# Normed inputs of every stage: two tiles to an instruction on VectorE, scale and shift on ScalarE

## The reference

```python
def rms_norm(x, g):
    xf = x.astype(jnp.float32)
    y = xf * lax.rsqrt(jnp.mean(xf * xf, axis=-1, keepdims=True) + RMS_EPS)
    return (y * g.astype(jnp.float32)).astype(x.dtype)

def modulate(h, shift, scale):
    return h * (1 + scale[:, None, :]) + shift[:, None, :]
...
        h = modulate(rms_norm(x, norm_ffn1[l]), sh1, sc1)
        x = x + 0.5 * g1[:, None, :] * swiglu(h, ffn1_w_in[l], ffn1_w_out[l])
        h = modulate(rms_norm(x, norm_mix[l]), sh2, sc2)
        x = x + g2[:, None, :] * token_mix(h, cos, sin, mix_w_in[l], sgu_w[l], sgu_b[l], mix_w_out[l])
        h = modulate(rms_norm(x, norm_ffn2[l]), sh3, sc3)
        x = x + 0.5 * g3[:, None, :] * swiglu(h, ffn2_w_in[l], ffn2_w_out[l])
```

## Time and profile before

| | us |
|---|---|
| median of 3 runs | 2261.4 (2260.69 to 2261.54) |
| the profiled execution | 2257.29 |
| its span, first to last instruction | 2255.2 |
| TensorE busy | 2108.4 (93%) |
| VectorE busy | 1689.1 (75%) |
| ScalarE busy | 988.7 (44%) |

### The profile page before, as it was taken

How to read it: one execution, slowest core, us unless ns; L and a number is a source line. 1 busy time by engine, 2 the same in 40 slices (tenths; PEclk the granted TensorE clock), 3 DMA queues, 4 the chain that set the end, 5 groups by cost and what they waited for, 6 DMA issues and landing times.

```text
span 2255.2 us, 35615 instructions
## 1 busy us (share of the span) xinstructions
PE 2108.4 (93%) x15149; PEld 1947.6 (86%) x15149; DVE 1689.1 (75%) x2346; ACT 988.7 (44%) x1325; POOL 28.2 (1%) x33
## 2 busy tenths in 40 slices
PE   5999898999999999999999899999999998678998
PEld 4999887999999998799998678888888886568998
DVE  7899877788788876778776774777776667966664
ACT  3434444433343444453345664422222358754442
POOL 0000000000000000000000000000000001110000
PEclk7999998999999999999999999999999999888998
DMA  9899743698879965357774001255565141133662
GB/s 320 286 326 307 245 150 112 221 309 301 290 259 304 312 200 168 131 185 249 240 227 153 28 20 57 94 168 168 168 212 178 60 130 61 36 110 127 215 201 75
DMA packets 338629, 417.43 MB, mean 185 GB/s; under 512 B 9274, under 2 KB 263208, under 8 KB 338472
## 3 DMA queue, kind: packets, MB, share of 16 engines
q1 hardware_dynamic: 335072, 410.79, 55.2%
q10 hardware_dynamic: 3400, 4.38, 0.6%
HBM read 414.09 MB, written 1.05 MB: 184 GB/s over the span
## 4 chain that ended last, share of the span: by engine, by line
PE 45%; DVE 7%; ACT 3%; issue 2%; POOL 0%; DVEq 0%; ACTq 0%
PE pb L600 44%; ACT wh L1323 1%; DVE wl L1926 1%; DVE RS L2013 1%; PE pb L1168 1%; DVE ACC L1934 1%; DVE SM L2510 1%; DVE T L1934 1%; DVE L_y L1934 0%; DVE Hl L1934 0%; ACT A_P L1780 0%; DVE L_u L1934 0%; DVE Y L1934 0%; DVE T L1926 0%; DVE L_y L1926 0%
## 5 line engine op out<-in xcount | busy, mean ns | idle before, releaser
L600 PE MATMUL pb<-Hh,wh 128*128 128x256 f32 (+1 forms) x2624 | 797.3, 304 | 32.1 <-DVE Hl L1934 20.0
L600 PE MATMUL pb<-Hl,wh 128*128 128x256 f32 (+1 forms) x2624 | 782.1, 298 | 0.0
L600 PE MATMUL pb<-Hh,wl 128*128 128x256 f32 (+1 forms) x2624 | 781.8, 298 | 0.0
L1926 DVE TENSOR_TENSOR wl<-raw,wh 128x2048 fp32r<-128x2048 f32 (+3 forms) x271 | 601.3, 2222 | 198.0 <-ACT wh L1323 197.3
L1323 ACT ACTIVATE wh<-raw 128x2048 fp32r<-128x2048 f32 (+3 forms) x271 | 502.5, 1855 | 358.2 <-PE pb L600 285.9
L600 PEld LDWEIGHTS pb<-Hh,wh 128*128 128x128 f32 x2624 | 506.7, 193 | 52.4 <-issue 28.5
L600 PEld LDWEIGHTS pb<-Hl,wh 128*128 128x128 f32 x2624 | 506.6, 193 | 15.0 <-issue 2.2
L600 PEld LDWEIGHTS pb<-Hh,wl 128*128 128x128 f32 x2624 | 506.5, 193 | 12.8
L600 PE MATMUL pb<-Bh,wh 128*128 128x256 f32 (+1 forms) x1376 | 419.8, 305 | 7.5 <-DVE Y L1926 2.5
L600 PE MATMUL pb<-Bh,wl 128*128 128x256 f32 (+1 forms) x1376 | 413.1, 300 | 0.0
L600 PE MATMUL pb<-Bl,wh 128*128 128x256 f32 (+1 forms) x1376 | 413.1, 300 | 0.0
(11 more groups left out here) (245 smaller groups left out, 2003.3 us busy)
## 6 DMA issues: line engine op xcount, KB each, us to landing
raw<-in_ada_w_dram SPq DMA_DIRECT2D x128, 1024.0 KB, 5.6
raw<-in_ffn_w_in_dram SPq DMA_DIRECT2D x88, 1024.0 KB, 6.1
raw<-in_mlp_w_dram SPq DMA_DIRECT2D x64, 1024.0 KB, 5.3
raw<-in_ffn_w_out_dram SPq DMA_DIRECT2D x32, 1024.0 KB, 6.9
raw<-in_mix_w_in_dram SPq DMA_DIRECT2D x22, 1024.0 KB, 5.9
raw<-in_ffn_w_out_dram SPq DMA_DIRECT2D x16, 768.0 KB, 5.4
raw<-in_attn_w_qkv_dram SPq DMA_DIRECT2D x12, 1024.0 KB, 6.3
raw<-in_lru_w_in_dram SPq DMA_DIRECT2D x10, 1024.0 KB, 5.1
```

Source lines behind the costliest of these rows:

```text
L600: return e.matmul(o, l, r, start=st, stop=sp, skip_group_check=True)
L1926: return e.tensor_tensor(o, a, b, f)
```

## The change

`modulated` now works on pairs of tiles. VectorE multiplies two tiles of XC by RS in one instruction (RS is broadcast over the two). ScalarE then applies scale (the gain) and shift to each tile of T in place, one instruction each with two per-partition operands, and makes one high-half copy for both. VectorE subtracts that from T, one instruction for both, and raises h by 2. ScalarE's copy waits for ScalarE's own second instruction of the pair (act.step). Where no other work stands beside the tiles, the copy for tiles 2 and 3 is put off until tiles 4 and 5 are scaled, and the next one likewise. The callers now hand the gain to ScalarE's side. The form with two segments in one call, which had no caller left, is dropped. The eight context tiles of the first feed-forward stage (`c_high`, `c_low`) are as before.

```diff
-            def modulated(segs, apart=False, beside={}):
...
-                    E.wait_ge("h.t", E.up("h.t"))
-                    act(Hh[:, kt, c], T[:, kt, c], ACT.Identity, bias=b[:, kt:kt + 1]).then_inc(sems["h.hi"], 1)
-                E.up("h", len(order))
+            def modulated(c0, a, b, beside={}):
+                c, done = slice(c0, c0 + 256), []
+
+                def high():
+                    kt, v = done.pop(0)
+                    E.wait_ge("act.step", v)
+                    act(Hh[:, kt:kt + 2, c], T[:, kt:kt + 2, c], ACT.Copy).then_inc(sems["h.hi"], 1)
+
+                for kt in range(0, 8, 2):
+                    for k in (kt, kt + 1):
+                        for f in beside.get(k, ()):
+                            f()
                     E.wait_ge("h.t", E.up("h.t"))
+                    for k in (kt, kt + 1):
+                        v = E.step(act(T[:, k, c], T[:, k, c], ACT.Identity, bias=b[:, k:k + 1], scale=a[:, k:k + 1]))
+                    done.append((kt, v))
+                    if kt != 2 or beside:
+                        high()
+                while done:
+                    high()
+                E.up("h", 8)
...
-            def modulated(segs, apart=False):
...
-                    stt(Hl[:, kt, c], T[:, kt, c], b[:, kt:kt + 1], f32(Hh[:, kt, c]), ALU.add, ALU.subtract).then_inc(sems["h"], 1)
+            def modulated(c0):
+
+                c, waiting = slice(c0, c0 + 256), []
+                r = RS[:, c].unsqueeze(1).to_broadcast([128, 2, 256])
 
                 def low():
-                    kt, c, b, k = waiting.pop(0)
+                    kt, k = waiting.pop(0)
                     E.wait_ge("h.hi", k)
+                    tt(Hl[:, kt:kt + 2, c], T[:, kt:kt + 2, c], f32(Hh[:, kt:kt + 2, c]), ALU.subtract).then_inc(sems["h"], 2)
 
                 own()
...
-                    stt(T[:, kt, c], XC[:, kt, c], a[:, kt:kt + 1], RS[:, c], ALU.mult, ALU.mult).then_inc(sems["h.t"], 1)
-                    waiting.append((kt, c, b, E.up("h.hi")))
-                    if len(waiting) > 2:
+                for kt in range(0, 8, 2):
+                    tt(T[:, kt:kt + 2, c], XC[:, kt:kt + 2, c], r, ALU.mult).then_inc(sems["h.t"], 1)
+                    waiting.append((kt, E.up("h.hi")))
+                    if kt > 2:
                         low()
```

More of the change, by code:

```diff
@@ L1373, in root_mean @@
                     act(RS[:, c0:c0 + 256], p[:, c0:c0 + 256], ACT.Sqrt, bias=EPSC, scale=1.0 / D).then_inc(sems["rs.sqrt"], 1)
-            def modulated(segs, apart=False, beside={}):
-                order = [(kt, s) for kt in range(8) for s in segs] if not apart else [(kt, s) for s in segs for kt in range(8)]
-                for kt, (c0, b) in order:
-                    for f in beside.get(kt, ()):
-                        f()
-                    c = slice(c0, c0 + 256)
-                    E.wait_ge("h.t", E.up("h.t"))
-                    act(Hh[:, kt, c], T[:, kt, c], ACT.Identity, bias=b[:, kt:kt + 1]).then_inc(sems["h.hi"], 1)
-                E.up("h", len(order))
+            def modulated(c0, a, b, beside={}):
[8 more added lines that the diff above has]
+                            f()
+                    E.wait_ge("h.t", E.up("h.t"))
+                    for k in (kt, kt + 1):
[6 more added lines that the diff above has]
+                E.up("h", 8)
             def shift(b, v, l, s):
@@ L1425, in ffn @@
                     cx_ahead()
-                modulated([(0, shift(0, 0, l, seg))])
+                modulated(0, S_GAIN, shift(0, 0, l, seg))
                 if first:
@@ L1472, in mix @@
                     cx_ahead()
-                modulated([(0, shift(0, 0, l, 3))])
+                modulated(0, S_GAIN, shift(0, 0, l, 3))
                 if l:
@@ L1619, in root, with seam @@
                 act(RS[:, SEG[seg]], PB[bank][:, SEG[seg]], ACT.Sqrt, bias=EPSC, scale=1.0 / D).then_inc(sems["rs.sqrt"], 1)
-            def seam(second, b_x, b_c, squared, beside, between, behind=()):
+            def seam(second, x, c, squared, beside, between, behind=()):
                 root(SUMS_BANK, 0)
@@ L1718, in _ @@
             cx_ahead()
-            modulated([(0, shift(1, 1, 0, 0))])
+            modulated(0, S_GX, shift(1, 1, 0, 0))
             cx_ahead()
@@ L1822, in _ @@
             E.wait_ge("xn", 8)
-            seam(SUMS2[0], shift(1, 1, 0, 3), shift(1, 2, 0, 3), {3: (o2_out(4, 1),), 6: (lambda: ahead("o2"),)},
+            seam(SUMS2[0], (S_MX, shift(1, 1, 0, 3)), (S_MC, shift(1, 2, 0, 3)), {3: (o2_out(4, 1),), 6: (lambda: ahead("o2"),)},
                  {2: (lambda: ahead("m1"),), 4: (o2_out(6, 1),), 5: (o2_squares(1, 4, 5),), 6: (o2_squares(1, 6, 7),)},
@@ L1826, in _ @@
             mlp(512, [2] * 8, halves=True)
-            seam(SUMS2[1], shift(1, 1, 1, 0), shift(1, 2, 1, 0), {5: (lambda: ahead("m2"),)},
+            seam(SUMS2[1], (S_LX, shift(1, 1, 1, 0)), (S_LC, shift(1, 2, 1, 0)), {5: (lambda: ahead("m2"),)},
                  {2: (lambda: ahead("lg"),), 4: (y_squares(1, 0, 1),), 5: (y_squares(1, 2, 3),)},
@@ L1910, in _ @@
             root_mean(256)
-            modulated([(0, shift(1, 1, 1, 3))])
+            modulated(0, S_GC, shift(1, 1, 1, 3))
             mlp(256, [4] * 4)
@@ L2069, in ffn @@
                     mean_root(256)
-                modulated([(0, S_GAIN, shift(0, 0, l, seg))])
+                modulated(0)
                 if seg or l:
@@ L2130, in mix @@
                 mean_root(256)
-                modulated([(0, S_GAIN, shift(0, 0, l, 3))])
+                modulated(0)
                 if l:
@@ L2341, in y_half, with seam @@
                     E.mark(tt(y, y, p[:, :].rearrange("p (m n) -> p m n", m=2), ALU.add), "y")
-            def seam(gates, x, c, added, between, behind=()):
+            def seam(gates, added, between, behind=()):
                 add_normed(256, [(0, gates[0])])
@@ L2446, in _ @@
             mean_root(256)
-            modulated([(0, S_GX, shift(1, 1, 0, 0))])
+            modulated(0)
             cx()
@@ L2566, in _ @@
             gain(S_MC, 1, 2, 0, 3, ng(0, 2))
-            seam((S_OX, S_OC), (S_MX, shift(1, 1, 0, 3)), (S_MC, shift(1, 2, 0, 3)), (lambda: ahead("o2"),), (lambda: ahead("m1"),))
+            seam((S_OX, S_OC), (lambda: ahead("o2"),), (lambda: ahead("m1"),))
             mlp(512, [2] * 8, halves=True)
@@ L2572, in _ @@
             gain(S_LC, 1, 2, 1, 0, ng(1, 0))
-            seam((S_GX, S_GC), (S_LX, shift(1, 1, 1, 0)), (S_LC, shift(1, 2, 1, 0)), (lambda: ahead("m2"), lambda: y_half(0, 1)),
+            seam((S_GX, S_GC), (lambda: ahead("m2"), lambda: y_half(0, 1)),
                  (lambda: y_half(4, 1), lambda: ahead("lg"), lambda: ahead("lg")), (lambda: ahead("lg"), lambda: ahead("lg")))
@@ L2674, in _ @@
             mean_root(256)
-            modulated([(0, S_GC, shift(1, 1, 1, 3))])
+            modulated(0)
             mlp(256, [4] * 4)
```

15 lines of the change are left out of this document (4 added, 11 removed).

## The result

The changed kernel takes 2286.36 us (median of 4 runs, 2282.09 to 2290.98) against 2261.05 for the kernel before (4 runs, 2260.45 to 2261.54): a ratio of 1.0116, 95% interval 1.0104 to 1.0128. That is 25.3 us slower; 2286.7 had been predicted. The profiled execution is the slowest of the four: 2290.98, span 2288.9, so the trace shows 33.7 us more than the trace of before and not 25.3. The other three spans are 2280.0, 2280.4 and 2288.1.

A forecast was written before the change was run, and what follows sets the result against it. TensorE, busy 93%, was taken as the bound: only its waits and slowdowns count. Call terms 4.3 + 6.2 + 5.5 + 9.3 = 25.3 us, added to the median 2261.4, gave 2286.7; range 2273 to 2297.

The forecast's parts named there:

- What bounds the kernel: Whole kernel: TensorE is busy 93% of the span, so a microsecond counts only where it stands still or slows.
- The new rhythm: Each call: ScalarE sets the pace, holding 6.1 us; at 626 first tile 1.54 later, unit's end 2.3 later.
- low bound: All twelve calls with the scale operand free and no clock loss: together 17.4 us, 2279.
- TensorE's gap before the third tile: Call at 626: TensorE through two tiles at 4.80, then idle 1.06 until 5.86 after the first T.
- 418, 626, 977: Calls with TensorE at full clock, where the unit's end counts: 1.6, 2.3 and 2.3 us, sum 6.2.
- 39, 270, 2048: Calls with TensorE at half clock: start counts at the last two, ScalarE's queue at 39; 1.3, 1.5, 1.5, sum 4.3.
- 836, 1192, 1426, 1826: Calls where a later wait swallows TensorE's delay and its releaser sits behind VectorE or ScalarE: 1.4, 1.4, 1.4, 1.3, sum 5.5.
- 1401 and 1792: First halves of the seams: ScalarE's other work joins the chain; 4.5 and 4.8 us including half the clock loss, sum 9.3.
- Rival 3: Clock falls at 418, 626, 836, 977, 1192 and 1426, each with a 1.2 GHz spell: 2300, +39; chance 0.05.
- Busy times: Profile after: ScalarE's busy time rises by about 39 us, VectorE's falls by 26 us.
- The weighed page: Skill page on ScalarE: about 93 ns per per-partition operand, spacing 0.51 instead of 0.49, some 0.15 us more a call.
- Rival 2: All 12 calls: VectorE's time is what counts, 1.4 us less work each, so faster, 2244; chance 0.04.

The follow-up runs named there:

- the execution shown first: First profiled execution of the changed kernel, no further edit, set beside a second profiled execution of the same kernel: 2290.98 us, span 2288.9.
- the tile-by-tile kernel: Changed kernel with ScalarE's two passes kept, but each tile of 256 columns handled singly without waiting for a partner: 2281.86 us, ratio 1.0088.

## Why the prediction was right, and where it was not

- **What bounds the kernel: right.** VectorE's lighter load moved nothing; every delay is a wait for a tile or for what is queued behind it.
- **The new rhythm: right, to 0.06 us in all five times of the call at 626.** ScalarE holds some 6.1 us a call. The second operand measures 0.092 (588 to 496) against 0.09. The spacing of 0.49 that came from it was the term on which most hung, and the kernel without scale moved the total to +17.6 where the low bound had 17.4. Call by call it bears the terms out at 418, 626, 977 and 1401 (0.9, 1.7, 1.7, 3.2 against 1.0, 1.7, 1.7, 3.3), while 836 was 3.3 over its term and 270 2.2 under: the closeness of the total is partly luck.
- **TensorE's gap before the third tile: 0.74, not 1.06.** I had it through two tiles 1.44 after the start. By its rows it is through at 639.06 - 0.74 - 636.66 = 1.66, since the last matmul ends later than its successor could begin. No effect on the unit's end, 10.30.
- **418, 626, 977 (1.6, 2.3, 2.3): right**, 1.51, 2.34, 2.35, and 2.34 each where they stood alone.
- **39, 270, 2048 (1.3, 1.5, 1.5): the mechanism is half of it.** The first tile is 1.6 later, but the price is not. Clock at 2048, in the kernel before and in the changed one, from TensorE's first tile on:

```profile
2050.00:2053.00 3.00, 2.71 (x13) 2.75 (x14) 3.00 (x9) 1.87 (x5) 0.00 (x0) 0.50 0.00 0
2053.00:2055.00 2.00, 2.00 (x11) 2.00 (x11) 1.89 (x5) 1.72 (x3) 0.00 (x0) 0.50 0.00 0
2055.00:2057.00 2.00, 2.00 (x16) 2.00 (x16) 0.92 (x1) 1.05 (x1) 0.00 (x0) 0.83 0.00 0
```

```profile
2083.00:2086.00 3.00, 1.32 (x6) 1.36 (x7) 1.44 (x3) 2.97 (x7) 0.00 (x0) 0.50 0.00 0
2086.00:2088.00 2.00, 2.00 (x11) 2.00 (x11) 0.86 (x2) 2.00 (x5) 0.00 (x0) 0.50 0.00 0
2088.00:2090.00 2.00, 2.00 (x17) 2.00 (x16) 1.12 (x2) 2.00 (x2) 0.00 (x0) 0.88 0.00 0
```

  Full clock comes back 7.2 us after the first T in both (at about 2055.7 and 2088.5), whether TensorE began 1.8 or 3.4 after it. Who begins 1.6 later works 1.6 less at half clock and gets 0.7 back: 0.91, not 1.5. At 270 a refund of 0.4 is in the rows (from the first tile to the next wait 20.7 before, 20.3 now), and then two spells, from about 296 and from about 306, take some 2.9 (4.06 less the 1.2 by which that wait comes later): I had no term for them. At 39 the measured values, 1.4, 0.1 and 3.2, allow no verdict.
- **836, 1192, 1426, 1826 (1.4, 1.4, 1.4, 1.3): delay right at three, price too low.** At 1192 TensorE waits for wl until 10.13 after T where it was 8.69, which is my 1.4, and VectorE is free at 7.79, not 6.34. But the wait grew from 1.81 to 3.26 with it, and half clock behind it costs another 1.4 or, in the execution shown first, 4.2 (it has a second spell at 1300 that the other lacks). At 1826 likewise: L_g at 10.97 instead of 9.75, 1.2 as laid out, then the spell. At 1426 it cost 1.5 without a spell: TensorE reaches Bl at 22.22 after T instead of 20.78, 1.4 as laid out. With one it cost 2.5 to 2.7; that spell lies in the call's own matmuls and makes TensorE so late that the wait for Bl is gone. At 836 the path was wrong. I had the wait for SM swallow TensorE's delay; it is 1.34 in both kernels and comes as a whole 1.9 later:

```profile
868.61 0.36 PE L600 MATMUL pb<-Hh,wh 128*128 128x256 f32 x1 [1.34 <-DVE SM L2206]
```

  That is 22.89 after T instead of 21.01. In other executions 836 cost 4.6. That can't be laid to the change, for with the call in its old form the stretch once cost 2.8. The step that failed, at 1192 and 1826: I priced the grown waits by their length alone, and gave clock loss behind them to a rival with 0.05.
- **1401 and 1792 (4.5, 4.8): too high by 0.7 and 0.8.** The laid-out pairs came when they should (fourth at 11.86, laid out 12.1); the unit ended at 13.39, laid out 13.6. The half share of clock loss that I added to each was not there: the clock is at half while TensorE is starved, and whole again for the later pairs.
- **The sum.** Terms too high by about 0.7 + 0.8 + 0.6; not in it were spells and the 0.5 at 836, worth some 9 to 11 in the two traced executions (33.7 and 32.1 less 25.3, plus the 2.1) and less in the two that were 8 us shorter. In the median of the first four runs the errors about cancel; on another chip the same kernel was 29.5 over. So 25.3 against 25.3 is closer than the working deserved, and 22 to 30 is what it was worth. Rival 3 was thus not one case of its own but a part of both traced executions, at four or five places (270, 1192, 1426, 1826, once 836) of which only three are among its six.
- **Busy times: ScalarE +30.2, not +39; VectorE -14.3, not -26.** I multiplied counts by mean durations. The page counts overlapping instructions once: 16 x 0.40 held before, 8 x 0.61 now, is 1.5 a call or 18 us in all, still more than was measured; my own spacing had said so.
- **The weighed page.** The Trainium skill, "ScalarE: Activation LUTs" under "What ACT_TABLE_LOAD costs", has about 93 ns for a per-partition operand; the runs here show 92 (496 to 588). The spacing is 0.49, as my sum had it and not the 0.51 worked out from that page: four in 2.06 us in the call at 626.
- **Rival 2.** Its rows set unlike instructions side by side (481 and 693). Like for like, VectorE's subtraction takes 424 ns for 256 columns in the tile-by-tile kernel and 691 for 512 here. So two tiles at once do save VectorE time, and still the pairs made the kernel slower (29.5 against 20.6 on one chip).
